# Two weight units in one DMA of 1 MB in the plain sets of the FFN's gate/up pairs

## The chip, the cores and the metric

One core of one Trainium2 chip. The metric is the time of one execution on the device, in microseconds (us), as the median of several runs.

## The reference, cut to what matters

One hybrid decoder layer in float32 on 256 tokens of width 2048: an input projection, a Mamba-2 branch and a differential-attention branch, an output projection, and then a SwiGLU FFN with a hidden width of 5632. The change lies in the FFN:

```
h = rms_norm(x, ffn_norm_w)                                   # 256 x 2048
a = silu(h @ w_ffn_gate) * (h @ w_ffn_up)                     # 256 x 5632, weights 2048 x 5632
x = x + a @ w_ffn_down                                        # weights 5632 x 2048
```

The weights are float32 in HBM and each is read once.

## The kernel before, in words

**A weight unit.** All weights stream through one pipeline in units of 256 rows x 512 columns (512 KB in float32, two tiles of 128 rows). SyncE's queue (SP) loads a unit by one DMA (`load`, L327 to L336, issued at L334) into one of four raw slots `w_raw[:, r]`. ScalarE (ACT) copies the slot rounded to the matmul's format (`w_hi`, L784 in the FFN's pairs, L463 elsewhere). VectorE (DVE) takes the remainder `w_lo = w_raw - w_hi` (L1306 in the pairs, L847 elsewhere). TensorE (PE) then multiplies: a plain unit is 12 matmuls (2 row tiles x 2 token tiles x the three products hi*hi, hi*lo, lo*hi) at L1500. `w_hi` and `w_lo` have four slots each.

**What orders it.** Each engine runs its own program in order, and semaphores tie them. ACT waits for the slot's DMA (`raw_in[r]`, one semaphore for each raw slot, +16 for each DMA) and for PE to have finished the unit four before (`mm_done`). DVE waits for ACT (`hi_ready`). PE waits for DVE (`lo_ready`). A raw slot is free once DVE has taken its remainder, so the next load into it waits for that count of `lo_ready`:

```
sp.wait_ge(lo_ready, unit.now(1 - RING))      # RING is 4: all but the last three units before this one are split
```

**The FFN's first half.** There are 11 pairs, one for each 512 columns of the hidden width; a pair computes both gate and up for its columns. It has 16 raw units, in four sets of four. Sets 0, 1 and 3 are plain: gate, gate, up, up for 512 rows of the weights, and 4 plain units of PE work. Set 2 (`SEVEN`) is done in Strassen's manner: its four raw units are turned into seven operands, three of them direct copies and four of them sums that DVE writes into the raw slots (`weights_sum`, L1311), and PE runs six matmuls for each of the seven (L1870). A pair therefore has 19 operands (`OPERANDS`) for 16 raw units. This text numbers the raw units of a pair q0 to q15 (q8 to q11 are set 2, q12 to q15 set 3), and its operands 0 to 18: 0 to 7 are q0 to q7, 8 to 14 the seven products, 15 to 18 are q12 to q15. A further operand n0, n1, ... is one of the next pair. The seven operands take raw slots 0, 3, 2, 0, 1, 2, 3 in order (`RAW_SLOT`), so slot 0 is read for the last time by operand 11, slot 1 by operand 12, slot 2 by operand 13 and slot 3 by operand 14. q12 to q15 go to slots 0, 1, 2, 3 again. On DVE the four sums stand between the remainders: one after operand 8, two after operand 10, one after operand 11.

After PE's third unit of a pair come eight transposes (L1516) for the products of the pair before; the evacuations and the silu of a pair lie on DVE (L1342 to L1364) and ACT (L806 to L812) in set 3 and the first set of the next pair.

**Second half.** `w_ffn_down` streams in 4 chunks of 22 plain units, with the same pipeline.

Of the kernel before, what the change touches and what calls it, by code (L numbers as in the profile page):

```python
# [32 lines left out]
P = 128  # L33
T = 256
TT = T // P
D = 2048
# [5 lines left out]
G = 8  # L42
# [7 lines left out]
FF = 5632  # L50
KF = FF // P
CW = 512
CT = CW // P
UK = 2
RING = 4
LEAD = 4
UPC = KD // UK
# [9 lines left out]
RAWS = 4 * SETS  # L67
# [3 lines left out]
OPERANDS = RAWS + len(PRODUCTS) - 4  # L71
RAW_SLOT = (0, 3, 2, 0, 1, 2, 3)
S1, S2, S3, S4 = 0, 1, 2, 3

COL_Z = 0
COL_X = DI
# [76 lines left out]
def layer(nc, x, mix_norm_w, w_in, conv_w, conv_b, dt_bias, a_log, d_skip, ssm_norm_w, w_ssm_proj,  # L153
# [3 lines left out]
    with ctx:  # L157
# [10 lines left out]
        w_raw = at("w_raw", 0, [P, RING, UK, CW])  # L168
# [100 lines left out]
        raw_in = [sem(f"raw_in{r}") for r in range(RING)]  # L269
        hi_ready = sem("hi_ready")  # L270
        lo_ready = sem("lo_ready")
        mm_done = sem("mm_done")
# [51 lines left out]
        def _(sp):  # L324
            unit = Tally()

            def load(source, row_tile, col):  # L327

                r = unit.slot % RING
                if not (unit.n < RING and isinstance(unit.base, int)):  # L330

                    sp.wait_ge(lo_ready, unit.now(1 - RING))
                src = source[0, row_tile * P:(row_tile + UK) * P, bass.ds(col, CW)]
                sp.dma_start(w_raw[:, r], src.rearrange("(k p) n -> p k n", p=P)).then_inc(raw_in[r], 16)  # L334
                unit.step()

            def chunk(source, col, units=UPC):
                for u in range(units):
                    load(source, u * UK, col)
# [39 lines left out]
            for n, first in enumerate((COL_BC, COL_GA)):  # L379
                with repeat(sp, 2, [(unit, 2 * UPC)]) as i:  # L380
                    for c in range(2):
                        for u in range(UPC):
                            if u in (4, 5):
# [4 lines left out]
                                src = qk[:, :, bass.ds(i * 4 + head, 1)].rearrange("p w o t d -> p w (o t) d")  # L388
# [21 lines left out]
            with repeat(sp, FF // CW, [(unit, OPERANDS)]) as i:  # L410
                for s in range(SETS):
                    first, second = 2 * UK * s, 2 * UK * s + UK
                    if s == SEVEN:

                        for source, row in ((w_ffn_gate, first), (w_ffn_up, first), (w_ffn_up, second), (w_ffn_gate, second)):
                            load(source, row, i * CW)
                        unit.n += OPERANDS - RAWS
                    else:
                        for source, row in ((w_ffn_gate, first), (w_ffn_gate, second), (w_ffn_up, first), (w_ffn_up, second)):
                            load(source, row, i * CW)  # L420

            def store(c):

# [3 lines left out]

            for c in range(D // CW):
                for u in range(KF // UK):
                    load(w_ffn_down, u * UK, c * CW)  # L430
                    if c and u == KF // UK // 2:
                        store(c - 1)
            c = D // CW - 1
# [9 lines left out]
        def _(act):  # L443
# [9 lines left out]
            nc.scalar.sem_inc(acc_free[0], 1)  # L453
            nc.scalar.sem_inc(acc_free[1], 1)

            def split_hi(extra=0, held=RING):

                s, r = unit.n - extra, unit.slot % RING
                act.wait_ge(raw_in[r], unit.base * (16 // RING) + 16 * (s // RING + 1))
                if not (isinstance(unit.base, int) and s < RING):  # L460

                    act.wait_ge(mm_done, unit.now(1 - held))
                nc.scalar.activation(w_hi[:, r], w_raw[:, r], ACT.Copy).then_inc(hi_ready, 1)  # L463
                unit.step()

# [285 lines left out]

            for c in range(4):
                for u in range(UPC):
                    split_hi()
                    if c == 0 and u == 2:
                        merged_hi(3)
                    if c and u == 3:
                        residual_hi(c - 1)
# [8 lines left out]
            def operand_hi(i, at):  # L767

                if at == OPERANDS:
                    unit.slot = 0  # L770
                if FIRST7 <= at < AFTER7:
                    n = at - FIRST7
                    source = RAW_SLOT[n]
                    if n < 3:
                        act.wait_ge(raw_in[source], raw.now(RAWS // 2) * (16 // RING) + 16)
                    else:
                        act.wait_ge(weights_summed, i * 4 + (n - 2))
                else:
                    nth = at if at < FIRST7 else at - (OPERANDS - RAWS)
                    source = nth % RING  # L780
                    act.wait_ge(raw_in[source], raw.now(nth - source) * (16 // RING) + 16)
                held = RING if at < OPERANDS else (3, 3, 3, 7)[at - OPERANDS]
                act.wait_ge(mm_done, unit.now(1 - held))
                nc.scalar.activation(w_hi[:, unit.slot % RING], w_raw[:, source], ACT.Copy).then_inc(hi_ready, 1)  # L784
                unit.step()
# [34 lines left out]


            for n in range(4 * (KF // UK) - LEAD):
                split_hi(unit.n - LEAD - n - raw.n)
                if n == 2:
                    product_hi(FF // CW - 1)

# [7 lines left out]
        def _(dve):  # L834
# [478 lines left out]
            def ffn_pair(i, head):  # L1313
                for at in range(OPERANDS):
                    operand_lo(at + LEAD)
                    if head and at == 0:
                        stationary_sums()
                    if head and at == 2:
                        dve.wait_ge(s_hi_ready, 1)
                        nc.vector.tensor_tensor(s_lo[:], s_sum[:], s_hi[:].bitcast(F32), ALU.subtract).then_inc(s_lo_ready, 1)  # L1320
                    if head and at == 3:
                        residual_lo(D // CW - 1)
                    if not head and at == 3:
                        product_lo(i - 1)
                    if at == FIRST7 - LEAD:

                        dve.wait_ge(raw_in[1], raw.now(RAWS // 2) * (16 // RING) + 16)
                        weights_sum(0, 0, 1)
                    if at == FIRST7 - LEAD + 2:
                        weights_sum(1, 1, 2)  # L1330
                        dve.wait_ge(weights_summed, i * 4 + 2)
                        weights_sum(2, 0, 2)
                    if at == FIRST7 - LEAD + 3:
                        dve.wait_ge(weights_summed, i * 4 + 3)
                        weights_sum(3, 2, 3)
                    if at == AFTER7 - 2:

                        dve.wait_ge(mm_done, unit.now(-LEAD))
                        dve.wait_ge(p1_ready, i + 1)
                        if not head:  # L1340
                            dve.wait_ge(a_T, i)
                        link(nc.vector.tensor_tensor(up_f[:, 0], side[:, 1], gate_f[:, 0], ALU.subtract))  # L1342
                        link(nc.vector.tensor_tensor(up_f[:, 1], up_f[:, 0], side[:, 3], ALU.subtract))
                    if at == AFTER7 - 1:
                        nc.vector.tensor_tensor(up_f[:, 0], side[:, 0], up_f[:, 0], ALU.add)
                        nc.vector.tensor_tensor(gate_f[:, 1], side[:, 0], up_f[:, 1], ALU.add).then_inc(mids_free, 1)
                    if at == AFTER7:
                        dve.wait_ge(mm_done, unit.now(1 - LEAD))
                        nc.vector.tensor_tensor(gate_f[:, 0], acc[0][:, 0], gate_f[:, 0], ALU.add)
                        nc.vector.tensor_tensor(up_f[:, 1], acc[0][:, 1], up_f[:, 1], ALU.subtract).then_inc(gates_summed, 1)  # L1350
                        dve.wait_ge(gates_summed, i + 1)
                        nc.vector.sem_inc(acc_free[0], 1)
                    if at == OPERANDS - 2:
                        dve.wait_ge(mm_done, unit.now(1 - LEAD))
                        dve.wait_ge(mids_free, i + 1)
                        nc.vector.tensor_tensor(up_f[:, 0], acc[1][:, 0], up_f[:, 0], ALU.add)
                        link(nc.vector.tensor_tensor(gate_f[:, 1], acc[1][:, 1], gate_f[:, 1], ALU.add))
                        nc.vector.sem_inc(acc_free[1], 1)
                if head:
                    dve.wait_ge(x2_rstd, 1)  # L1360
                dve.wait_ge(gate_f_ready, i + 1)
                nc.vector.scalar_tensor_tensor(out=up_f[:, 0], in0=up_f[:, 0], scalar=x2_scale[:, 0:1], in1=gate_f[:, 0],
                                               op0=ALU.mult, op1=ALU.mult)
                nc.vector.scalar_tensor_tensor(out=up_f[:, 1], in0=gate_f[:, 1], scalar=x2_scale[:, 1:2], in1=up_f[:, 1],  # L1364
                                               op0=ALU.mult, op1=ALU.mult).then_inc(a_ready, 1)
                raw.step(RAWS)
# [599 lines left out]
```

## Time and profile before

| | |
|---|---|
| median of 3 runs | 2089.68 us (2089.66 to 2090.87) |
| the profiled execution | 2089.39 us, of which the span from the first to the last instruction is 2087.7 us |
| granted TensorE clock, mean | 0.999 |
| busy, share of the span | PE 100%, weight loads 82%, DVE 66%, ACT 51%, GpSimd 7% |
| data moved by DMA | 394.46 MB, mean 189 GB/s |

The profile is of one execution. A row of the timeline gives the start, the duration (from the first start to the last end, where several are merged), the engine, the line of the kernel and the tiles. Matmuls overlap, so PE's durations of one matmul are longer than the time between two. Times are from the span's start.

### The profile page before, as it was taken

The numbers are of one execution on the slowest core, as the hardware profiler recorded it, in microseconds if no ns is written. First come the engines' busy times: TensorE is split into PE (matmuls) and PEld (weight loads), VectorE is DVE, ScalarE is ACT, GpSimd is POOL, SyncE is SP. The second block draws the span as 40 slices with busy tenths as digits, with TensorE's granted clock in tenths as the row PEclk, the third lists the DMA queues.
The fourth block names the chain that finished last, engine by engine and source line by source line (L and its number), as shares of the span: only waits on it lengthen the run. The fifth ranks groups of instructions, "written<-read, shape, count | busy, mean of one in ns | idle before, by whom it ended". The sixth has DMA issues, their size and how long they took to land.

```text
span 2087.7 us, 28374 instructions
## 1 busy us (share of the span) xinstructions
PE 2079.0 (100%) x9658; PEld 1715.0 (82%) x9658; DVE 1372.1 (66%) x1677; ACT 1072.2 (51%) x1380; POOL 144.5 (7%) x174
## 2 busy tenths in 40 slices
PE   9999999999999999999999999999999999999999
PEld 7888877778888888888888888888888888888887
DVE  6676456665767777777664555577777887764443
ACT  5444455554566666666654444455555555543333
POOL 1121000000012222222000000000000000000000
PEclk9999999999999999999999999999999999999999
DMA  7656665554565555555575555556656666566554
GB/s 237 205 177 209 197 198 169 163 176 138 189 204 172 189 186 185 183 182 181 171 231 193 191 189 187 189 176 197 201 161 198 205 199 202 161 223 205 199 200 141
DMA packets 207541, 394.46 MB, mean 189 GB/s; under 512 B 15665, under 2 KB 21218, under 8 KB 207218
## 3 DMA queue, kind: packets, MB, share of 16 engines
q1 hardware_dynamic: 204530, 384.79, 56.7%
q0 software_dynamic: 2336, 8.46, 1.3%
q8 instruction: 40, 0.66, 0.1%
q10 hardware_dynamic: 608, 0.34, 0.1%
q14 instruction: 27, 0.22, 0.0%
HBM read 387.18 MB, written 2.16 MB: 186 GB/s over the span
## 4 chain that ended last, share of the span: by engine, by line
PE 93%; DVE 3%; issue 2%; DMA 1%; ACT 1%; DVEq 0%; SPq 0%; ACTq 0%
PE acc L1500 84%; PE side L1516 3%; PE side L1870 2%; DVE w_raw L1311 1%; PE side L1743 1%; DVE w_lo L1306 1%; PE acc L1870 1%; PE side L1598 1%; ACT w_hi L784 1%; DMA w_raw<-in_w_in 0%; DMA x_row<-in_x 0%; PE side L1749 0%; PE acc L1516 0%; PE side L1672 0%; DVE w_lo L847 0%
## 5 line engine op out<-in xcount | busy, mean ns | idle before, releaser
L847 DVE TENSOR_TENSOR w_lo<-w_raw,w_hi 128x1024 fp32r<-128x1024 f32 x536 | 668.2, 1257 | 538.0 <-ACT w_hi L463 537.1
L463 ACT ACTIVATE w_hi<-w_raw 128x1024 fp32r<-128x1024 f32 x536 | 564.0, 1058 | 708.0 <-PE acc L1500 651.9
L1500 PE MATMUL acc<-w_hi,h_hi 128*128 128x512 f32 x1280 | 511.4, 400 | 0.1
L1500 PE MATMUL acc<-w_hi,h_lo 128*128 128x512 f32 x1280 | 499.9, 391 | 0.0
L1500 PE MATMUL acc<-w_lo,h_hi 128*128 128x512 f32 x1280 | 498.8, 390 | 0.0
L784 ACT ACTIVATE w_hi<-w_raw 128x1024 fp32r<-128x1024 f32 x209 | 220.2, 1060 | 211.5 <-PE acc L1500 120.9
L1306 DVE TENSOR_TENSOR w_lo<-w_raw,w_hi 128x1024 fp32r<-128x1024 f32 x209 | 252.6, 1223 | 96.1 <-ACT w_hi L784 89.9
L1500 PEld LDWEIGHTS acc<-w_hi,h_hi 128*128 128x128 f32 x1280 | 240.7, 188 | 52.5 <-issue 5.5
L1500 PEld LDWEIGHTS acc<-w_hi,h_lo 128*128 128x128 f32 x1280 | 240.5, 188 | 51.5
L1500 PEld LDWEIGHTS acc<-w_lo,h_hi 128*128 128x128 f32 x1280 | 241.0, 188 | 49.3 <-issue 1.9
L1500 PE MATMUL acc<-w_hi,x2T_hi 128*128 128x512 f32 x528 | 206.7, 391 | 0.1
L1500 PE MATMUL acc<-w_hi,x2T_lo 128*128 128x512 f32 x528 | 205.6, 389 | 0.0
L1500 PE MATMUL acc<-w_lo,x2T_hi 128*128 128x512 f32 x528 | 205.5, 389 | 0.0
L1500 PE MATMUL acc<-w_hi,a_hi 128*128 128x512 f32 x348 | 135.5, 389 | 0.0
L1500 PE MATMUL acc<-w_hi,a_lo 128*128 128x512 f32 x348 | 135.4, 389 | 0.0
L1500 PE MATMUL acc<-w_lo,a_hi 128*128 128x512 f32 x348 | 135.4, 389 | 0.0
L1500 PEld LDWEIGHTS acc<-w_hi,x2T_hi 128*128 128x128 f32 x528 | 99.1, 188 | 21.1 <-issue 1.0
L1500 PEld LDWEIGHTS acc<-w_hi,x2T_lo 128*128 128x128 f32 x528 | 99.1, 188 | 20.7
L1500 PEld LDWEIGHTS acc<-w_lo,x2T_hi 128*128 128x128 f32 x528 | 99.2, 188 | 20.2
L1500 PE MATMUL acc<-w_hi,y_hi 128*128 128x512 f32 x256 | 99.9, 390 | 0.0
L1500 PE MATMUL acc<-w_hi,y_lo 128*128 128x512 f32 x256 | 99.6, 389 | 0.0
L1500 PE MATMUL acc<-w_lo,y_hi 128*128 128x512 f32 x256 | 99.6, 389 | 0.0
(276 smaller groups left out, 2352.2 us busy)
## 6 DMA issues: line engine op xcount, KB each, us to landing
w_raw<-in_w_in SPq DMA_DIRECT2D x320, 512.0 KB, 4.2
w_raw<-in_w_ffn_gate SPq DMA_DIRECT2D x88, 512.0 KB, 3.7
w_raw<-in_w_ffn_up SPq DMA_DIRECT2D x88, 512.0 KB, 4.5
w_raw<-in_w_ffn_down SPq DMA_DIRECT2D x88, 512.0 KB, 3.5
w_raw<-in_w_ssm_proj SPq DMA_DIRECT2D x64, 512.0 KB, 4.2
w_raw<-in_w_attn_proj SPq DMA_DIRECT2D x32, 512.0 KB, 3.5
w_raw<-in_w_out SPq DMA_DIRECT2D x32, 512.0 KB, 3.5
acs_b<-acs_scratch POOLq DMA_DIRECT2D x16, 512.0 KB, 7.1
```

The lines of the kernel that those rows point to most:

```text
L463: nc.scalar.activation(w_hi[:, r], w_raw[:, r], ACT.Copy).then_inc(hi_ready, 1)
L784: nc.scalar.activation(w_hi[:, unit.slot % RING], w_raw[:, source], ACT.Copy).then_inc(hi_ready, 1)
L847: nc.vector.tensor_tensor(w_lo[:, r], w_raw[:, r], w_hi[:, r].bitcast(F32), ALU.subtract).then_inc(lo_ready, 1)
L1306: nc.vector.tensor_tensor(w_lo[:, r], w_raw[:, source], w_hi[:, r].bitcast(F32), ALU.subtract).then_inc(lo_ready, 1)
L1311: return nc.vector.tensor_tensor(w_raw[:, at], w_raw[:, one], w_raw[:, other], ALU.add).then_inc(weights_summed, 1)
L1500: done = nc.tensor.matmul(acc[p][:, t], a[:, k0 + kk, cut], w[:, r, kk], start=first and kk == n == 0, stop=last and kk == UK - 1 and n == 2)
L1516: return nc.tensor.transpose(out_at, in_, ident)
L1598: last = nc.tensor.matmul(side[:, 1 + m, first:first + width], qkT[half, 0, q * P:(q + 1) * P], qkT[half, 1, 0:width], start=True, stop=True)
L1743: nc.tensor.matmul(side[:, t, cut], decay[:, h, t], xdt[:, t, cut], start=True, stop=True)
L1870: done = nc.tensor.matmul(out_at, a, w[:, r, kk], start=first and kk == n == 0, stop=last and kk == UK - 1 and n == 2)
```

## The change

In the plain sets the four loads of 512 KB become two loads of 1 MB: gate rows of both units into slots 0 and 1, up rows of both into slots 2 and 3. Set 2 keeps its four loads. So that the per-slot semaphores keep constant offsets, the first four units of `w_ffn_down` are loaded by two such DMAs too; all other loads stay. A load of two waits for both slots, and it raises only the semaphore of the first (0 or 2); ACT waits on that one for either unit. The waits on slots 1 and 3 elsewhere are given new counts.

```diff
+            def load_two(source, row_tile, col):
+
+                r = unit.slot % RING
+                sp.wait_ge(lo_ready, unit.now(2 - RING))
+                src = source[0, row_tile * P:(row_tile + 2 * UK) * P, bass.ds(col, CW)]
+                both = w_raw[:, r:r + 2].rearrange("p r k n -> p (r k) n")
+                sp.dma_start(both, src.rearrange("(k p) n -> p k n", p=P)).then_inc(raw_in[r], 16)
+                unit.step(2)
+
...
                     else:
-                        for source, row in ((w_ffn_gate, first), (w_ffn_gate, second), (w_ffn_up, first), (w_ffn_up, second)):
-                            load(source, row, i * CW)
+                        for source in (w_ffn_gate, w_ffn_up):
+                            load_two(source, first, i * CW)
...
-                    load(w_ffn_down, u * UK, c * CW)
+                    if c or u >= RING:
+                        load(w_ffn_down, u * UK, c * CW)
+                    elif u % 2 == 0:
+                        load_two(w_ffn_down, u * UK, c * CW)
...
-                    act.wait_ge(raw_in[source], raw.now(nth - source) * (16 // RING) + 16)
+                    act.wait_ge(raw_in[source - source % 2], raw.now(nth - source) * (16 // RING) + 16)
...
-                        dve.wait_ge(raw_in[1], raw.now(RAWS // 2) * (16 // RING) + 16)
+                        dve.wait_ge(raw_in[1], i * 16 + (PLAIN_UNITS * (16 // RING) + 16))
```

## Rows read from the trace of the kernel before

**Rows 1.** The page: busy time by engine, and the chain's shares
```profile
PE 2079.0 (100%) x9658; PEld 1715.0 (82%) x9658; DVE 1372.1 (66%) x1677; ACT 1072.2 (51%) x1380; POOL 144.5 (7%) x174
...
PE 93%; DVE 3%; issue 2%; DMA 1%; ACT 1%; DVEq 0%; SPq 0%; ACTq 0%
```

**Rows 2.** Busy time by stretch: all pairs; then one pair
```profile
core 0: us, PE busy (x) PEld busy (x) DVE busy (x) ACT busy (x) POOL busy (x), PEclk, DMA share, GB/s
1372.00:1853.20 481.20, 480.30 (x2147) 394.24 (x2147) 384.64 (x383) 256.89 (x264) 1.38 (x3) 1.00 0.60 192
1592.00:1635.46 43.46, 43.41 (x197) 35.69 (x196) 34.50 (x35) 22.71 (x24) 0.00 (x0) 1.00 0.59 193
```

**Rows 3.** Waits in the pairs, 1372 to 1853.2: total, times, longest
```profile
ACT w_hi L784 <- DMA w_raw<-in_w_ffn_gate: 61.1, 38, 3.4
ACT w_hi L784 <- DMA w_raw<-in_w_ffn_up: 21.1, 22, 1.7
...
PEld side L1870 <- DVE w_lo L1306: 5.5, 11, 0.6
```

**Rows 4.** The chain that ended last, in the sixth pair
```profile
1603.44 1.07 ACT w_hi L784
...
1611.62 3.02 PE side L1870 x12
1614.64 1.36 PE acc L1870 x6
1616.00 19.04 PE acc L1500 x84
```

**Rows 5.** Timeline of SP: set 3's loads, sixth pair; then last pair
```profile
1609.46 0.37 SPq L334 DMA_DIRECT2D w_raw<-in_w_ffn_gate  x1
...
1611.73 0.37 SPq L334 DMA_DIRECT2D w_raw<-in_w_ffn_gate  x1
...
1612.73 0.37 SPq L334 DMA_DIRECT2D w_raw<-in_w_ffn_up  x1
...
1613.87 0.37 SPq L334 DMA_DIRECT2D w_raw<-in_w_ffn_up  x1
...
1826.75 0.37 SPq L334 DMA_DIRECT2D w_raw<-in_w_ffn_gate  x1
1829.02 0.37 SPq L334 DMA_DIRECT2D w_raw<-in_w_ffn_gate  x1
```

**Rows 6.** Timeline of ACT: operands 9, then 15 to 18, sixth pair
```profile
1601.22 1.06 ACT L784 ACTIVATE w_hi<-w_raw 128x1024 fp32r<-128x1024 f32 x1 [2.15 <-DMA w_raw<-in_w_ffn_gate]
...
1612.92 1.06 ACT L784 ACTIVATE w_hi<-w_raw 128x1024 fp32r<-128x1024 f32 x1 [1.32 <-DMA w_raw<-in_w_ffn_gate]
1615.38 1.06 ACT L784 ACTIVATE w_hi<-w_raw 128x1024 fp32r<-128x1024 f32 x1 [1.39 <-DMA w_raw<-in_w_ffn_gate]
1617.68 1.06 ACT L784 ACTIVATE w_hi<-w_raw 128x1024 fp32r<-128x1024 f32 x1 [1.24 <-DMA w_raw<-in_w_ffn_up]
1619.37 1.06 ACT L784 ACTIVATE w_hi<-w_raw 128x1024 fp32r<-128x1024 f32 x1 [0.62 <-DMA w_raw<-in_w_ffn_up]
```

**Rows 7.** Timeline of DVE, sixth pair: operands 9, 10; 12 to 16; n0
```profile
1602.31 1.23 DVE L1306 TENSOR_TENSOR w_lo<-w_raw,w_hi 128x1024 fp32r<-128x1024 f32 x1 [0.85 <-ACT w_hi L784]
1604.54 1.23 DVE L1306 TENSOR_TENSOR w_lo<-w_raw,w_hi 128x1024 fp32r<-128x1024 f32 x1 [1.00 <-ACT w_hi L784]
...
1610.35 3.49 DVE L1306 TENSOR_TENSOR w_lo<-w_raw,w_hi 128x1024 fp32r<-128x1024 f32 x3
1614.02 1.23 DVE L1306 TENSOR_TENSOR w_lo<-w_raw,w_hi 128x1024 fp32r<-128x1024 f32 x1 [0.18 <-ACT w_hi L784]
1616.47 1.23 DVE L1306 TENSOR_TENSOR w_lo<-w_raw,w_hi 128x1024 fp32r<-128x1024 f32 x1 [1.22 <-ACT w_hi L784]
...
1623.79 1.22 DVE L1306 TENSOR_TENSOR w_lo<-w_raw,w_hi 128x1024 fp32r<-128x1024 f32 x1
```

**Rows 8.** Busy time by half microsecond: PE clock, DMA share, GB/s last
```profile
1610.50:1611.00 0.50, 0.50 (x4) 0.42 (x3) 0.50 (x1) 0.46 (x1) 0.00 (x0) 1.00 0.67 131
...
1618.00:1618.50 0.50, 0.50 (x4) 0.42 (x3) 0.00 (x0) 0.50 (x1) 0.00 (x0) 1.00 1.04 397
1618.50:1619.00 0.50, 0.50 (x3) 0.40 (x3) 0.23 (x1) 0.24 (x1) 0.00 (x0) 1.00 1.07 414
```

**Rows 9.** The page's DMA issues, and line L334's landing in the pairs
```profile
x<-in_x SPq DMA_DIRECT2D x1, 2048.0 KB, 8.9
...
DMA to landing us min/median/max: 3.3/4.4/6.1
```

More of the change, by code:

```diff
@@ L73 @@
 S1, S2, S3, S4 = 0, 1, 2, 3
+PLAIN_UNITS = UPC * (7 * D // CW + 2 * G) + 3 * UPC * D // CW
 COL_Z = 0
@@ L454, in _, with split_hi @@
             nc.scalar.sem_inc(acc_free[1], 1)
-            def split_hi(extra=0, held=RING):
+            def split_hi(extra=0, shared=0, two=False):
                 s, r = unit.n - extra, unit.slot % RING
-                act.wait_ge(raw_in[r], unit.base * (16 // RING) + 16 * (s // RING + 1))
+                act.wait_ge(raw_in[r - r % 2 if two else r], unit.base * (16 // RING) + 16 * (s // RING + 1) - (shared if r % 2 else 0))
                 if not (isinstance(unit.base, int) and s < RING):
-                    act.wait_ge(mm_done, unit.now(1 - held))
+                    act.wait_ge(mm_done, unit.now(1 - RING))
                 nc.scalar.activation(w_hi[:, r], w_raw[:, r], ACT.Copy).then_inc(hi_ready, 1)
@@ L753, in _ @@
                 for u in range(UPC):
-                    split_hi()
+                    split_hi(two=c == D // CW - 1 and u >= UPC - LEAD)
                     if c == 0 and u == 2:
@@ L774, in operand_hi @@
                     if n < 3:
-                        act.wait_ge(raw_in[source], raw.now(RAWS // 2) * (16 // RING) + 16)
+                        if source % 2:
+                            act.wait_ge(raw_in[source], i * 16 + (PLAIN_UNITS * (16 // RING) + 16))
+                        else:
+                            act.wait_ge(raw_in[source], raw.now(RAWS // 2) * (16 // RING) + 16)
                     else:
@@ L822, in _ @@
             for n in range(4 * (KF // UK) - LEAD):
-                split_hi(unit.n - LEAD - n - raw.n)
+                split_hi(unit.n - LEAD - n - raw.n, 16 * (3 * FF // CW + 1))
                 if n == 2:
```

## The prediction, made blind

> **What bounds the kernel now.** I read the page first: PE is busy for 2079.0 of 2087.7 us and the chain that ended last is 93% PE [rows 1]. The stage that is edited, the eleven pairs, lasts 481.20 us with 480.30 us of PE work, the clock at its upper level of 2.4 GHz (granted share 1.00) throughout, and a single pair has 43.41 us of PE work in 43.46 [rows 2]. So nothing that frees SP, ACT or DVE can pay here by itself: PE's idle time in the whole stage is 0.9 us. Then I read the waits: ACT waits 60 times for a raw unit's DMA, 82.2 us in sum, while PE's only wait worth a row is 5.5 us, 0.5 in each pair, before the fifth of the seven products [rows 3]. The reader is to see two things. The DMAs are already late for ACT, and that costs nothing as long as the split units stay ahead of PE. And the lead they have must be read place by place, for it is the only thing that pays for a later load. I therefore followed one pair in time, the sixth, on SP, ACT, DVE and PE [rows 4 to 7].
>
> **Where the lead is smallest.** Raw slots 0 to 3 are read until operands 11 to 14, in the middle of the seven products, where each operand takes PE only 1.36 us [rows 4] and DVE has four sums besides. q12 is issued at 1609.46 and q13 at 1611.73 [rows 5]. ACT starts on q12 at 1612.92, as soon as it has landed (3.46 us after issue) [rows 6]; DVE's remainder is from 1614.02 to 1615.25 [rows 7]; PE wants that unit at 1616.00, with no gap in its chain [rows 4]. The lead there is 0.75 us. For q13 it is 1.03 us (1617.70 against 1616.00 + 2.73, where 2.72 to 2.73 us is a plain unit: 19.04 us for 84 matmuls, twelve to a unit) [rows 4, 7]. For the next pair's first unit it is 1.9 us (1625.01 against 1616.00 + 4 x 2.73) [rows 4, 7].
>
> **The change part by part.**
>
> *Issues saved.* Each pair issues 10 loads in place of 16, and the start of the down projection two fewer. An issue occupies SP's sequencer for 0.37 us [rows 5], SP is otherwise waiting for slots, and nobody waits for SP's time itself: 0 us.
>
> *Later issue for the first of two.* The load of q12 and q13 must wait until slot 1 is free too, which is DVE's remainder of operand 12. DVE has operands 12, 13 and 14 back to back from 1610.35 to 1613.84 [rows 7], so operand 12 ends at about 1611.58, and the joint load goes out where q13 went out, at 1611.73: 2.27 us later than q12 did [rows 5]. Nothing moves this point forward: it hangs on DVE's row of remainders and sums that starts with PE's and ACT's event at 1603.44 [rows 4].
>
> *Longer transfer.* ACT may not touch q12 before the whole 1 MB is there. The trace before has no 1 MB load of this form, so the price is bounded. One unit alone takes 3.46 us to landing. From below: when the DMA engines are full they move 397 to 414 GB/s [rows 8], which is 1.3 us for the second 512 KB, so 4.8 us. From another form, the 2 MB load of x takes 8.9 us [rows 9]: (8.9 - 3.46) / 3 = 1.8 us for each further 512 KB, so 5.3. Units already queued behind each other land 2.30 us (q14 after q13) and 1.69 us (q15 after q14) apart [rows 6], so 5.2 to 5.8. From above, two loads one after the other: 3.46 + 3.46 = 6.9. I take 5.2 (1.7 us for the second half), as one DMA of the same pattern is nearest to the units that follow each other in the queue.
>
> A page bears on this price, beside the sum. The Trainium skill ("DMA: Bandwidth & Descriptors", section on the anatomy of one DMA) gives for loads issued from GpSimd a fixed 2.0 us and bytes over 436 GB/s; an estimate by it is 1.2 us for the second 512 KB, 4.7 us in all, and the sum below would be 5.5 us smaller. It agrees with the lower bound.
>
> *What it costs PE.* Issue 1611.73, landed and ACT started 1616.93 (+5.2), remainder started 1618.03 (+1.10, as 1612.92 to 1614.02), ended 1619.26 (+1.23), PE started 1619.30 (+0.04, as between DVE's end at 1611.58 and PE's row at 1611.62) [rows 4, 6, 7]. PE wanted 1616.00. The lead of 0.75 us is eaten and PE stands for 3.3 us. The last pair's loads have the same spacing (1826.75 and 1829.02) [rows 5], and I found the same in all eleven. The stall cannot be hidden by a longer lead in the pair before, because DVE cannot split into slots that PE has not freed: the chain of the seven operands starts from PE's own progress. Sum: 11 x 3.3 = 36 us.
>
> *q14 and q15.* Issued together when operand 14 is split, 1613.87, where q15 was [rows 5, 7]. They queue behind the first megabyte and land by about 1620.3. ACT and DVE then have operand 17 ready by 1622.6 and, after DVE's two evacuations, operand 18 by about 1625.2. PE, late by now, wants them at 1619.3 + 5.45 = 1624.8 and at 1627.5. Covered by 2 us: 0. If that cover is gone the price is the excess, once in each pair.
>
> *The next pair's sets 0 and 1.* n0 and n1 go out together when operand 16 is split, about 1620.5, and land at 1625.7; n0 is ready at 1628.0 and PE wants it at 1630.2: covered by 2.2 us. In steady plain units the joint load goes out 2.4 us after a unit of PE ends, takes 5.2, and ACT wants it 3 x 2.73 = 8.2 us after that end: 0.6 us ahead even of ACT, and PE wants it later by three more units. So sets 0 and 1, the first pair's start behind the output projection, and the first four units of the down projection cost 0.
>
> *Set 2.* Its loads keep their form. q11 needs slot 3, which operand 7 frees, and operand 7 hangs on PE's fourth unit, not on a DMA, so q11 is issued as early as now relative to PE. But q10 now goes out about 2 us later than it did, close ahead of q11, and may push q11's landing back by up to 0.9 us. ACT starts operand 9 on q11's landing at 1601.22 and its next at 1603.44, DVE ends operand 9 at 1603.54 and starts the next at 1604.54 [rows 4, 6, 7]: 1.0 us of cover, so 0, with little to spare. If q11 is later still, the excess goes straight into the row of sums and is paid eleven times.
>
> Sum: 2089.4 (the profiled execution, 2087.7 of span and 1.7 around it) + 36 = 2125.7; the median of the runs shown is 0.3 us above that execution, so **2126 us**, 1.7% slower.
>
> **The rivals.**
>
> 1. *Dearer transfer, or a second stall.* The joint load takes 6.9 us (two loads in a row): a stall of 5.0 us, 55 us in all, 2145. Or q11's landing slips past its 1.0 us of cover by 1 to 2 us: 11 to 22 us more, 2137 to 2148. For it: landings in the pairs reach 6.1 us, median 4.4 [rows 9], so loads that follow each other do stretch. Against: one unit alone lands in 3.5, and full engines move 400 GB/s. Chance 0.13.
>
> 2. *Cheaper stall.* The second half costs 1.3 us or less, and PE stands for 2.9 us or less: 2121 and down. At 1.0 us it would be 2.6 us, 2118. This is inside my range; a time below 2115 would need under 0.75 us for 512 KB, about 700 GB/s, against 414 seen, or an earlier issue. Chance of below 2115: 0.05.
>
> 3. *Not slower: larger transfers use the engines better.* One DMA in place of two drops one start-up: traffic of q12 begins only about 1 us after its issue (131 GB/s in the stretch from 1610.5) [rows 5, 8]. If ACT got its data earlier by that everywhere, the 82.2 us of ACT's waits would shrink, and the 0.5 us wait of PE in each pair with them, at most 5.5 us: 2084. The place that decides is q12: PE keeps its pace only if the joint load lands within 5.2 - 3.3 = 1.9 us of its issue. The fastest landing of a half-size load is 3.3 us [rows 9]. Chance 0.03 for faster, and 0.02 for a cover that I have not seen which leaves it within 0.2%. The Trainium skill speaks for this rival ("DMA: Bandwidth & Descriptors", section with the rules for kernel authors: for most bandwidth, 128 partitions and at least 1 MiB in a DMA). The stage moves 192 GB/s with its DMA engines 60% busy [rows 2], so here bandwidth is not what is short; by that rule alone the time would not rise.
>
> **How the numbers follow.** The forecast (a stall of 2.3 to 4.7 us before set 3 in each pair, nothing else) has 0.77; rival 1 has 0.13, rival 2 below the range 0.05, rival 3 and its kin 0.05. The range goes from 2115 (a stall of 2.3 us, the second half at 0.75) to 2141 (11 x 4.7 us: the second half at 3.1, or at 2.3 with a second stall of 0.8), and leaves out half of rival 1. A measurement of this kernel can tell about 0.2% (4 us) from no change. Slower by more than that: 0.95; within it 0.02; faster 0.03.
>
> **What would show it.** In the new profile SP's joint load of set 3 goes out where operand 12's remainder ends, in every pair, as q13's did. ACT waits for DMA at operand 15 for some 5 us where it was 1.3. PE's chain shows ACT and DVE, behind a DMA of `w_ffn_gate`, between the last L1870 and the next L1500, about 3.3 us in each of eleven pairs, and a pair lasts 46.7 us in place of 43.5. Time to landing of the 1 MB loads is 4.8 to 5.8 us. PE's granted clock stays 1.00. Sets 0 and 1 and the down projection show no new wait of PE. I am wrong if the joint load is issued earlier than operand 12's end, if PE also waits at the seven products by more than the 0.5 us of before, or if ACT finds q12 landed.

## The result, and the profile after

The changed kernel takes 2148.47 us (median of 4 runs, 2145.52 to 2150.44) against 2089.67 us of the kernel before in the same rounds: a ratio of 1.028, with a 95% interval from 1.0263 to 1.0298. The direction and the place were forecast, the size was not: 2126 us was predicted and the range ended at 2141.

The page of the changed kernel, its first line, the busy times, the chain's shares and the 1 MB loads (with their median time to landing):

```profile
span 2143.9 us, 28151 instructions
...
PE 2099.2 (98%) x9658; PEld 1727.0 (81%) x9658; DVE 1372.2 (64%) x1677; ACT 1068.9 (50%) x1380; POOL 144.9 (7%) x174
...
PE 88%; DMA 4%; DVE 4%; issue 2%; ACT 2%; SPq 0%; DVEq 0%; ACTq 0%
...
w_raw<-in_w_ffn_gate SPq DMA_DIRECT2D x33, 1024.0 KB, 5.0
w_raw<-in_w_ffn_up SPq DMA_DIRECT2D x33, 1024.0 KB, 5.2
```

The reader is to see two things here. DMA has entered the chain, as forecast. And PE is busy for 2099.2 us where it was 2079.0 [rows 1], with the same 9658 matmuls: 20.2 us more for the same work. Nothing in the prediction makes a matmul slower.

The waits in the pairs (1372 to 1910) of the changed kernel:

```profile
ACT w_hi L800 <- DMA w_raw<-in_w_ffn_gate: 123.0, 32, 5.5
...
ACT w_hi L800 <- DMA w_raw<-in_w_ffn_up: 47.6, 21, 4.2
PEld acc L1516 <- DVE w_lo L1322: 40.4, 11, 3.9
PE acc L1516 <- DVE w_lo L1322: 35.7, 11, 3.4
PEld side L1886 <- DVE w_lo L1322: 6.4, 12, 1.0
```

Eleven waits of PE at L1516, 35.7 us in sum: 3.25 us each, where 3.3 was forecast and none was before [rows 3]. (The row of PEld is the same standstill seen by the weight load.) One of them in full, first SP's joint load, then ACT's and PE's row behind it, in the timeline of the fifth pair:

```profile
1586.47 0.37 SPq L344 DMA_DIRECT2D w_raw<-in_w_ffn_gate  x1
...
1591.67 2.00 ACT L800 ACTIVATE w_hi<-w_raw 128x1024 fp32r<-128x1024 f32 x2 [5.33 <-DMA w_raw<-in_w_ffn_gate]
...
1594.04 0.80 PE L1516 MATMUL acc<-w_hi,x2T_hi 128*128 128x512 f32 x1 [3.30 <-DVE w_lo L1322]
```

Issue to ACT's start is 5.20 us (1591.67 - 1586.47), and PE stands for 3.30. Those were the prediction's own numbers. What it lacked is in the last row's 0.80 us for one matmul, where it is 0.39 elsewhere. Busy time by stretch of the same place, with PE's granted clock as the third number from the right:

```profile
core 0: us, PE busy (x) PEld busy (x) DVE busy (x) ACT busy (x) POOL busy (x), PEclk, DMA share, GB/s
1586.47:1590.70 4.23, 4.23 (x18) 3.19 (x18) 2.11 (x2) 0.00 (x0) 0.00 (x0) 1.00 0.70 243
1590.70:1594.00 3.30, 0.04 (x1) 0.00 (x0) 1.24 (x2) 2.00 (x2) 0.00 (x0) 0.97 0.83 306
1594.00:1597.50 3.50, 3.46 (x9) 2.73 (x10) 2.15 (x2) 2.01 (x2) 0.00 (x0) 0.54 0.33 80
1597.50:1606.00 8.50, 8.50 (x39) 7.01 (x38) 7.21 (x10) 3.02 (x4) 0.00 (x0) 1.00 0.62 221
```

The clock was at its upper level while PE worked, fell in this pair at the end of the standstill, and PE's first 3.5 us back at work were granted 0.54 of 2.4 GHz, that is 1.2 GHz nearly throughout: 9 matmuls where the pace of the next row gives 16. Then it was back at 1.00. The chain shows the price pair by pair, because it has the seven units behind each standstill as one piece of 84 matmuls, 19.04 us before [rows 4]. After (the first pair's piece has only 36 matmuls):

```profile
1399.37 10.02 PE acc L1516 x36
...
1448.59 19.34 PE acc L1516 x84
...
1495.65 22.17 PE acc L1516 x84
...
1545.44 20.94 PE acc L1516 x84
...
1594.04 20.85 PE acc L1516 x84
...
1642.73 22.00 PE acc L1516 x84
```

19.34 is a standstill with no fall of the clock behind it (0.3 us to start again; PE had stood for 3.29 us there too); 20.9 is one fall; 22 us is a stay at the lower level about twice as long, and in those three pairs the fall began 0.8 to 1.1 us before PE was back at work, earlier than in any other. Of the ten long pieces one is 19.34, six are 20.77 to 20.95 and three 22.00 to 22.17. Their excess over 19.05 is 20.5 us, and 1.5 us more in the first pair (10.02 against 8.47 for 36 matmuls elsewhere). So of the 56 us that the profiled executions differ by (2145.52 against 2089.39), 36 are the standstill and about 22 the clock and the restart behind it; the pairs begin 2 us earlier than before, which closes the sum.

### The profile page after: what moved, and what is told of

Read it like the earlier page. It is cut to its first block, busy times and chain, and to the rows that moved or that the text cites. A ratio compares the mean times of both kernels' runs of the same rounds, so it can differ in the third digit from the quotient of the medians.

```text
span 2143.9 us, 28151 instructions
## 1 busy us (share of the span) xinstructions
PE 2099.2 (98%) x9658; PEld 1727.0 (81%) x9658; DVE 1372.2 (64%) x1677; ACT 1068.9 (50%) x1380; POOL 144.9 (7%) x174
## 4 chain that ended last, share of the span: by engine, by line
PE 88%; DMA 4%; DVE 4%; issue 2%; ACT 2%; SPq 0%; DVEq 0%; ACTq 0%
PE acc L1516 81%; DMA w_raw<-in_w_ffn_gate 3%; PE side L1532 3%; DVE w_lo L1322 2%; ACT w_hi L800 1%; PE side L1759 1%; DVE w_raw L1327 1%; PE side L1614 1%; DMA w_raw<-in_w_in 0%; DMA x_row<-in_x 0%; PE side L1765 0%; PE acc L1532 0%; DVE w_lo L863 0%; PE side L1688 0%; DMA w_raw<-in_w_ffn_up 0%
## 5 line engine op out<-in xcount | busy, mean ns | idle before, releaser
L1516 PE MATMUL acc<-w_hi,h_hi 128*128 128x512 f32 x1280 | 510.8, 399 | 0.1
L1516 PE MATMUL acc<-w_hi,h_lo 128*128 128x512 f32 x1280 | 499.6, 390 | 0.0
L1516 PE MATMUL acc<-w_lo,h_hi 128*128 128x512 f32 x1280 | 498.4, 389 | 0.0
L1516 PEld LDWEIGHTS acc<-w_hi,h_hi 128*128 128x128 f32 x1280 | 240.5, 188 | 52.1 <-issue 5.5
L1516 PEld LDWEIGHTS acc<-w_hi,h_lo 128*128 128x128 f32 x1280 | 240.3, 188 | 51.6
L1516 PEld LDWEIGHTS acc<-w_lo,h_hi 128*128 128x128 f32 x1280 | 240.7, 188 | 49.1 <-issue 1.9
L1516 PE MATMUL acc<-w_hi,x2T_hi 128*128 128x512 f32 x528 | 216.4, 410 | 35.7 <-DVE w_lo L1322 35.7
L1516 PE MATMUL acc<-w_hi,x2T_lo 128*128 128x512 f32 x528 | 212.6, 403 | 0.0
L1516 PE MATMUL acc<-w_lo,x2T_hi 128*128 128x512 f32 x528 | 212.4, 402 | 0.0
L1516 PEld LDWEIGHTS acc<-w_hi,x2T_hi 128*128 128x128 f32 x528 | 103.9, 197 | 61.9 <-DVE w_lo L1322 40.4
L1516 PE MATMUL acc<-w_hi,a_hi 128*128 128x512 f32 x348 | 135.5, 389 | 0.0
L1516 PE MATMUL acc<-w_hi,a_lo 128*128 128x512 f32 x348 | 135.4, 389 | 0.0
L1516 PE MATMUL acc<-w_lo,a_hi 128*128 128x512 f32 x348 | 135.4, 389 | 0.0
L1516 PEld LDWEIGHTS acc<-w_lo,x2T_hi 128*128 128x128 f32 x528 | 104.3, 198 | 21.6
L1516 PEld LDWEIGHTS acc<-w_hi,x2T_lo 128*128 128x128 f32 x528 | 103.3, 196 | 22.8
L1516 PE MATMUL acc<-w_hi,y_hi 128*128 128x512 f32 x256 | 99.9, 390 | 0.0
L1516 PE MATMUL acc<-w_hi,y_lo 128*128 128x512 f32 x256 | 99.6, 389 | 0.0
L1516 PE MATMUL acc<-w_lo,y_hi 128*128 128x512 f32 x256 | 99.6, 389 | 0.0
```

The lines of the kernel that those rows point to most:

```text
L1516: done = nc.tensor.matmul(acc[p][:, t], a[:, k0 + kk, cut], w[:, r, kk], start=first and kk == n == 0, stop=last and kk == UK - 1 and n == 2)
```

## The experiments

Eight kernels change which loads are joint, or their timing; three put filler work into the standstill or its place. In those that choose the joint loads the semaphore counts follow from a list of the joint loads (`TWOS`), so that only the loads and their waits differ. Times are medians; the ratio is to the kernel before in the same rounds.

**1. All joint loads but those of set 3.** `TWOS` holds sets 0 and 1.

```diff
-                        for source in (w_ffn_gate, w_ffn_up):
-                            load_two(source, first, i * CW)
+                        for half, source in enumerate((w_ffn_gate, w_ffn_up)):
+                            if (s, half) in TWOS:
+                                load_two(source, first, i * CW)
+                            else:
+                                load(source, first, i * CW)
+                                load(source, second, i * CW)
```

> The changed kernel, but set 3 of each pair loads its four units by four DMAs of 512 KB again; sets 0 and 1 and the start of the down projection keep the 1 MB loads. Theory A (all of the loss is in set 3: the joint load of q12 and q13 makes TensorE stand for about 3.3 us, and the clock granted after that standstill is the lower level for some 3.7 us, which costs 1.9 us more, 11 times): the time is that of the kernel before within 0.2%, 2086 to 2094 us, and the granted clock is 1.00 in all pairs. Theory B (only the standstill is set 3's, and the other 20 us come from the 1 MB loads of sets 0 and 1): about 2110 us.

Measured 2098.69 us, ratio 1.0049 (1.0032 to 1.0066), clock 1.00. About 50 of the 59 us are gone with set 3's joint loads, and the fall of the clock with them; but 9 us stay, more than theory A allowed. The chain of this kernel shows them as DMA pieces in a row, here around its sixth pair:

```profile
1577.40 5.18 DMA w_raw<-in_w_ffn_gate
...
1592.45 5.28 DMA w_raw<-in_w_ffn_up
...
1601.31 4.15 DMA w_raw<-in_w_ffn_gate
...
1614.98 3.92 DMA w_raw<-in_w_ffn_gate
```

These are q0+q1, q6+q7, q11 and q13, each issued when DVE ends the unit before it in the chain (its row stands between them). The joint loads of sets 0 and 1 thus push q11 back past the 1.0 us of cover that the prediction gave it. In the changed kernel this delay is hidden in set 3's larger one, for the kernel of experiment 2, which hasn't it, is as slow.

**2. Joint loads in set 3 alone.** `TWOS` holds set 3's two.

> The kernel before, with the 1 MB loads in set 3 alone (q12+q13 and q14+q15); sets 0 and 1 and the down projection load by 512 KB. Theory A (all of the loss is in set 3): 2089.7 + 11 x 5.1 = 2146 us, within 4 us of the changed kernel, the same 3.2 us standstill before operand 15 in each pair and the same stretch at the lower clock behind it. Theory B (sets 0 and 1 carry 20 us): about 2126 us.

Measured 2147.72 us, ratio 1.0279 (1.0262 to 1.0296), clock 0.988; the first waiting matmul of its fifth pair:

```profile
1594.49 0.80 PE L1532 MATMUL acc<-w_hi,x2T_hi 128*128 128x512 f32 x1 [3.34 <-DVE w_lo L1338]
```

As theory A had it. Set 3 makes the whole loss, and sets 0 and 1 add nothing to it.

**3. Later issue without longer transfers.** The kernel before, with this in the plain sets; the first four units of the down projection are loaded the same way:

```diff
-                    sp.wait_ge(lo_ready, unit.now(1 - RING))
+                    sp.wait_ge(lo_ready, unit.now(1 + both - RING))
...
+                        for source in (w_ffn_gate, w_ffn_up):
+                            load(source, first, i * CW, both=1)
+                            load(source, second, i * CW)
```

> The kernel before with its DMAs of 512 KB, but in the plain sets the first of two waits until both slots are free, as the joint load does; the second follows at once. It tells the later issue from the longer transfer. The first unit lands 3.5 us after 1611.7 in place of 5.0. Theory A1 (the standstill is additive, later issue 2.27 us less the lead of 0.75, and the clock falls only behind the long standstill): standstill 1.6 us, 11 x 1.6 = 18 us, 2107 us, clock 1.00. Theory A2 (a standstill of 1.6 us is already enough for the lower clock to follow): 11 x (1.6 + about 1.9) = 38 us, 2128 us. Theory C (two loads issued together share the engines, so the first lands no earlier than the joint one): 2146 us.

Measured 2127.91 us, ratio 1.0191 (1.0174 to 1.0208), clock 0.993. This is A2 in kind, and its 2128 us is met in part by luck: the standstill is longer than 1.6 us and the price behind it smaller than 1.9. The first unit is with ACT 4.17 us after its load's issue (issue 1578.72, ACT 1582.89), a little more than the 3.5 us of a unit alone, so the standstill is about 2 us (1.78 to 2.27) instead of 1.6: 21.8 us in eleven waits. The clock falls behind it too, to the same level. The chain of this kernel, and then its busy time by stretch:

```profile
1578.72 4.07 DMA w_raw<-in_w_ffn_gate
...
1582.89 1.06 ACT w_hi L785
...
1583.98 1.24 DVE w_lo L1307
...
1585.26 20.96 PE acc L1501 x84
```
```profile
1585.50:1589.00 3.50, 3.50 (x9) 2.70 (x9) 2.20 (x3) 2.05 (x2) 0.00 (x0) 0.51 0.44 100
1589.50:1600.00 10.50, 10.50 (x48) 8.69 (x47) 7.75 (x10) 5.26 (x6) 0.00 (x0) 1.00 0.58 178
```

Nine of its eleven pieces of 84 matmuls take 20.9 to 21.0 us, two 19.34. So the later issue, with the 0.7 us by which its first load is with ACT later (4.17 against 3.46), makes 38 of the 59 us: 22 by the standstill, and the other 16 by the clock and the restart behind it.

**4. The standstill filled with work.** The changed kernel, and after the seven products of each pair:

```diff
+                        pe.wait_ge(p1_ready, i + 1)
+                        for _ in range(14):
+                            nc.tensor.matmul(side[:, 2], s_hi[:, 0, 0], s_hi[:, 0:2].rearrange("p s k n -> p (s k n)"), start=True, stop=True)
```

> The changed kernel, and after the seven products of each pair TensorE does 14 more matmuls of 512 columns (about 3.2 us at 2.4 GHz) on values already there, into a bank that nobody reads then; their result is not used. They fill the time in which it stands in the changed kernel. Theory A (the lower clock follows from the standstill): the standstill's own time stays, as work, and the clock stays 1.00: 2089.7 + 11 x 3.3 = 2126 us, 20 us less than the changed kernel in spite of more work. Theory D (the matmuls of set 3 are slow for another reason, such as the megabyte that is written into SBUF beside them): no gain, 2146 to 2150 us, and the granted clock still falls after the products.

Measured 2129.26 us, ratio 1.0191 (1.0174 to 1.0208), clock 0.999. More work on PE makes the changed kernel 19 us faster, and theory D falls: the same loads, the same set 3, and its matmuls run at full pace. The chain, joint load to set 3:

```profile
1582.76 5.16 DMA w_raw<-in_w_ffn_gate
...
1588.02 1.07 ACT w_hi L800
...
1589.12 1.24 DVE w_lo L1322
...
1590.40 19.38 PE acc L1516 x84
```

All ten such pieces are 19.34 to 19.38 us.

**5. The same filler in the kernel before.**

> Control for the filler: the kernel before (512 KB loads everywhere) with the same 14 matmuls of 512 columns after the seven products of each pair, results unused. Here TensorE does not stand at that place, so they are plain extra work: 14 x 0.227 us = 3.2 us a pair, 11 x 3.2 = 35 us, less the 0.5 us wait that they do not touch: 2125 us. If the time equals that of the changed kernel with the filler (2129 us) within 4 us, the megabyte load costs nothing beyond the 3.2 us of TensorE's time that the standstill or the filler occupies. If the filler were free or much dearer (under 2110 or over 2140 us), the reading of the filler run as a clock effect would be wrong.

Measured 2121.64 us, ratio 1.0155 (1.0139 to 1.0172). PE's pieces are 19.04 or 19.05 us, and the filler is plain work of 33 us (35 was forecast). The changed kernel with filler is 7.6 us slower than this one, 4 had been allowed: its weight load still waits 6.8 us in eleven short waits behind the filler, and its pieces have the 0.3 us of restart. So the 1 MB loads cost a little beyond the standstill. The rest of the reading holds: filler is neither free nor dear.

**6. Only q12+q13 joint.**

> The kernel before with one joint load in each pair: q12+q13 of set 3 as 1 MB, all other loads 512 KB. Theory A (this one load makes the whole loss, through the standstill before operand 15 and the lower clock behind it): 2145 us, within 4 us of the changed kernel. Rival (the joint load of q14+q15 is needed too, it stretches the first or prolongs the stall): under 2135 us.

Measured 2149.33 us, ratio 1.0289 (1.0272 to 1.0306). One load a pair makes the whole loss, as theory A had it.

**7. All joint but q12+q13.**

> The changed kernel with only q12 and q13 loaded by 512 KB again; five of six joint loads stay. Theory A: no long standstill, clock 1.00. What stays is the small loss of the kernel with set 3 single (2098.7 us, 0.8 us a pair) plus whatever q14+q15 as one load adds: it lands at about 1619.2 in the sixth pair's time in place of 1617.7 for q14, operand 17 is then split at 1621.5 where TensorE wants it at 1621.45, so 0 to 1 us a pair: 2098 to 2110 us. Rival (q14+q15 is dear by itself, with a standstill and a fallen clock): over 2120 us.

Measured 2124.33 us (2121.59 to 2130.15), ratio 1.0165 (1.0149 to 1.0182), clock 0.996. A miss for theory A: 25 us more than the kernel with set 3 single, where 0 to 12 were allowed; the rival had over 2120. The joint load of q14 and q15 is dear by itself. In all eleven pairs it lands later than the 5.2 us that is the median of this kernel's joint loads, after 5.8 to 8.0 us; two lines of this kernel's chain:

```profile
1536.33 7.70 DMA w_raw<-in_w_ffn_up
...
1583.69 7.81 DMA w_raw<-in_w_ffn_up
```

The stretches of the second show a load that is late without full engines. Data flow at 341 GB/s until 1588.5, then there is a hole of a microsecond (DMA share 0.13) before traffic goes on, and the load lands at 1591.50. (The next pair's first joint load is issued at 1588.49, so the traffic behind the hole is at least in part its own.)

```profile
1586.50:1588.50 2.00, 2.00 (x11) 1.49 (x10) 1.23 (x1) 0.56 (x1) 0.00 (x0) 1.00 0.93 341
1588.50:1589.50 1.00, 1.00 (x6) 0.83 (x6) 0.00 (x0) 0.00 (x0) 0.00 (x0) 1.00 0.13 49
1589.50:1591.50 2.00, 1.89 (x9) 1.22 (x7) 0.00 (x0) 0.00 (x0) 0.00 (x0) 1.00 0.93 246
```

The trace marks the arrival of each load sixteen times, as its semaphore rises by 16, and these marks tell what is late. Of this load fourteen come from 1588.42 to 1588.96, 4.7 to 5.3 us after its issue, about when all sixteen of an ordinary joint load do; the last two come at 1589.83 and 1591.50. In each of the eleven pairs twelve of its sixteen are there after 5.4 us at the latest, and the last comes after 5.8 to 8.0 us. So it is not the load as a whole that is slow, but one to four of its sixteen parts, and ACT waits for the last.

This kernel also bears on the clock. PE stands in eight of its pairs for 1.8 to 2.7 us, and the clock falls behind four of these standstills (2.1 to 2.6 us) and not behind the other four (1.8 to 2.7 us). The longest of all is one without a fall; its row, and the busy time behind it:

```profile
1878.38 0.50 PE L1532 MATMUL acc<-w_hi,x2T_hi 128*128 128x512 f32 x1 [2.70 <-DVE w_lo L1338]
...
1878.38:1883.38 5.00, 5.00 (x22) 4.10 (x23) 4.84 (x7) 2.01 (x2) 0.00 (x0) 1.00 0.21 57
```

So the length of a standstill does not by itself decide whether the clock falls behind it.

**8. Half of the filler** (7 matmuls in the changed kernel).

> The changed kernel with 7 in place of 14 filler matmuls (1.6 us) after the seven products; TensorE then stands for about 1.7 us in each pair. If this shorter standstill is still followed by the lower clock as in the kernel with two late 512 KB loads (standstill 2.0 us, 2128 us where 2107 was forecast without the clock), the time is close to the changed kernel's, 2140 to 2148 us. If the clock stays up, it is 2126 to 2130 us, as with 14.

Measured 2134.52 us (2130.84 to 2136.48), ratio 1.0222 (1.0205 to 1.0239), clock 0.998 in the profiled execution. Between the two expectations. Its eleven waits sum to 19.6 us, 1.8 us each, and of its ten pieces of 84 matmuls eight take 19.34 to 19.38 us and two 20.92 and 20.98. After standstills of 1.8 us (1.6 to 2.0) that follow on filler, the clock fell twice in eleven; after those of 2.0 us in experiment 3, nine times in eleven. Whether the filler or the shorter standstill makes that difference, no run separates.

**9. Joint loads in set 1 alone.**

> The kernel before with joint loads in set 1 alone (q4+q5, q6+q7). Reading of the kernel with set 3 single: its 9 us come from a chain that starts with the joint load of q0+q1, goes on over q6+q7 and q11 and delays the seven products. With set 1 alone the joint load of q6+q7 goes out when operand 3 of the pair is split (1632.4 in the sixth pair's time), lands at 1637.7, and operand 7 is rounded at 1638.8, where TensorE's progress asks 1638.7. So q11 is late by 0.1 to 0.3 us and within its cover of 1.0: 2089 to 2093 us, clock 1.00. Rival (each joint load costs the same, 9 us over four of them): 2094 us.

Measured 2092.28 us (11 runs), ratio 1.0014 (1.0005 to 1.0023). The time is within the chain reading's range, but the rival's 2094 us lies within the interval too; experiment 10 decides against the rival.

**10. Joint loads in set 0 alone** (and in the first four units of the down projection).

> The kernel before with joint loads in set 0 alone (q0+q1, q2+q3, and the first four units of the down projection). Chain reading: operand n1 to n3 are split some 0.7 us later, TensorE has 2 us of lead there, and the single loads of set 1 recover it: 2089 to 2093 us. Rival (set 0 starts the loss by itself, since its lead behind the seven products is the next smallest, 1.9 us): 2096 to 2099 us, as with both sets.

Measured 2090.35 us (11 runs), ratio 1.0004 (0.9995 to 1.0013): no difference, where equal prices for each joint load would give 2094 us. Apart, the two sets lose 0.18% together, in one kernel 0.49%. So the 9 us of experiment 1 need both: what set 0 delays, set 1's single loads recover, if the chain reading is right.

**11. Only q14+q15 joint.**

> The kernel before with one joint load in each pair, q14+q15 of set 3. In the kernel with all but q12+q13 joint it took 5.2 to 8.0 us to land, being issued 2.1 us behind q13 while that one was in flight, and TensorE stood for about 2 us in most pairs. If that belongs to this load: 2110 to 2122 us, and its landing is again 5.8 to 8 us. If it came from the late joint loads of sets 0 and 1 beside it: under 2100 us.

Measured 2106.51 us (2102.52 to 2109.55), ratio 1.0077 (1.0063 to 1.0091), clock 0.999. A miss: 3.5 us less than the lower end of the forecast, though far above the 2100 of the other reading. Its landings (smallest, median and largest, the joint loads' line in the pairs) are the slow ones again:

```profile
DMA to landing us min/median/max: 5.2/5.9/6.9
```

Here too only the last few of the sixteen parts are late: twelve are there after 5.1 us in every pair. PE stands for 1.8 us at most, and the clock falls in none of the pairs. So this load alone costs 17 us; with the joint loads of sets 0 and 1, which cost 9 us without it, it makes 35 (experiment 7), and there the clock falls in four pairs.

## Why the prediction was wrong, point by point

- **Where the lead is smallest: right.** Set 3's first unit, 0.75 us. Experiments 2 and 6 have the whole loss with its joint load in place, and without set 3's joint loads only 9 us of it are left (experiment 1).
- **Later issue by 2.27 us, at the end of operand 12: right.** In the chain of the changed kernel the joint load hangs on operand 12's remainder (1585.09 to 1586.32, issue 1586.47).
- **Landing 5.2 us, lower bound 4.8, upper 6.9: right.** Measured 5.20 at that place (issue to ACT's start, as the 3.46 us of one unit), median 5.0 over the gate loads.
- **The standstill, 3.3 us and 36 us in sum: right.** Measured 3.25 and 35.7.
- **"PE's granted clock stays 1.00": the step that failed.** The sum ended with the standstill and had no term for what the clock does after it. It fell to 1.2 GHz for some 3.5 us in ten of eleven pairs, at 1.4 to 2.8 us each beyond the 0.3 us of restart: about 19 us, 22 with the restart, and a pair in which it falls lasts 48.5 to 49.8 us where 46.7 was forecast. Experiment 4 shows that this is caused by PE's standing and not by the loads: filled, the same loads give 2129 us, 3 us from the forecast. Experiment 3 shows the same fall with no 1 MB load in the kernel. The Trainium skill has the rule ("TensorE: Matmul & The Clock Gate", part 1, the HAM clock gate): a gate sets the clock by how busy the array has been recently, throttled is the default and activity releases it. The trace agrees as to PE's idling (granted 1.00 before the standstill, 0.54 behind it, 1.00 again later), and a lower clock should have been one of the rivals from the moment that a standstill of some microseconds was forecast. What a fall costs is in the rows of the changed kernel: 1.6 us where it is short (20.94 against 19.34).
- **q14 and q15, "covered by 2 us": right only behind the first standstill.** There PE is late itself. Without it the joint load costs 17 us (experiment 11).
- **Sets 0 and 1 "cost 0": right in the changed kernel** (experiment 2 is as slow as it), wrong without set 3's delay: 9 us. The weak point was named, q11's 1.0 us of cover; that it gives way when both sets are joint is experiment 1.
- **Rival 1** named a second stall as the way over 2137 us. The time got there, but not by it: PE's wait at the seven products is 6.4 us in sum against 5.5 before [rows 3], with one of 1.0 us among them. Its other half, a load as slow as two, did not come for q12 and q13 either (4.9 to 5.3 us in the chain).
- **Rival 3**, better use of the DMA engines: nothing of it shows. One start-up less for each pair of units gains nothing when nobody on the path waits for bandwidth.

Left open: why one to four of the sixteen parts of a joint load that is issued while a 512 KB load is in flight arrive up to 3 us behind the rest. No run separates the queue from the memory there. Open too is what besides a standstill's length decides whether the clock falls behind it.

## What to carry to other kernels

Before two loads are made one, look for the place where the slots come free latest against the consumer: the joint load starts when the last of its slots is free and serves its first consumer when the last byte is there, and both delays (here 2.3 and 1.7 us) are paid from the smallest lead in the loop (0.75 us), not from the usual one. When a change is forecast to make TensorE stand even for two or three microseconds, add the lower clock behind the standstill to the sum, as a term that comes in some of the cases; here it was about a third of the loss. Filler matmuls in the standstill are a cheap test of which part is the clock.

## What the runs showed of the hardware

- TensorE's granted clock fell to the lower level in 10 of 11 pairs behind standstills of 3.3 us (11 of 11 in experiment 6, 10 of 11 in experiment 2), in 9 of 11 behind 2.0 us (two 512 KB loads issued late), in 4 of 8 behind 1.8 to 2.7 us (experiment 7), in 2 of 11 behind 1.8 us that followed on filler, and in none of 11 behind waits of at most 0.34 us (experiment 4; 0.6 us on average as the weight load counts them). It stayed there for about 3.5 us mostly, and longer in three pairs of the changed kernel; of its four runs the fastest (2145.52 us) has a mean clock of 0.990 and the slowest (2150.44 us) 0.987.
- Behind a standstill the seven units take 0.3 us more than without one even where the clock stays up: 19.34 us after 3.29 us of standing, and 19.34 to 19.38 in experiment 4, where PE stands for 0.34 us at most, against 19.04.
- A 1 MB load of four 2 KB rows to each partition lands in 5.0 us (median). ACT starts on it 5.20 us after its issue, and 3.46 us after that of 512 KB alone: 1.7 us for the second half. Issued 2.1 us behind a 512 KB load it took 5.2 to 8.0 us, with most of its sixteen parts there after about 5 us and the last one to four late.
